# A streaming hybrid encoder step on one core: another way to turn and sum the conditioning half vectors of the feed-forward rounds

## The reference, cut to what matters

```
ada = (silu(c) @ w_ada + b_ada).reshape(B, 9, D)          # 9 sequences, D = 1024
x = x + 0.5 * ada[2] * SwiGLU1(modulate(rms(x), ada[0], ada[1]))
x = x + ada[5] * Mixer(modulate(rms(x), ada[3], ada[4]))
x = x + 0.5 * ada[8] * SwiGLU2(modulate(rms(x), ada[6], ada[7]))
y = modulate(rms(x), *(silu(c) @ w_ada_final + b_ada_final))
SwiGLU(x) = (silu(x @ w_gate) * (x @ w_up)) @ w_down       # inner width 2816
```

## Time and profile before

| | us |
|---|---|
| median of 3 runs | 2403.04 (2400.04 to 2405.37) |
| profiled execution, its own time | 2404.43 |
| profiled execution, span from first to last instruction | 2402.7 |
| TensorE busy | 2342.3 (97%) |
| VectorE busy | 1579.6 (66%) |
| ScalarE busy | 985.2 (41%) |
| GpSimd busy | 129.7 (5%) |
| mean granted TensorE clock | 0.987 of full |

### The profile page before, as it was taken

How to read it: one execution, slowest core, us unless ns; L and a number is a source line. 1 busy time by engine, 2 the same in 40 slices (tenths; PEclk the granted TensorE clock), 3 DMA queues, 4 the chain that set the end, 5 groups by cost and what they waited for, 6 DMA issues and landing times.

```text
span 2402.7 us, 31657 instructions
## 1 busy us (share of the span) xinstructions
PE 2342.3 (97%) x11530; PEld 2007.2 (84%) x11530; DVE 1579.6 (66%) x2530; ACT 985.2 (41%) x1701; POOL 129.7 (5%) x173
## 2 busy tenths in 40 slices
PE   6999999999999999999999999999999999999998
PEld 4677777787788787999999999997777788878887
DVE  5965665666666766655666565569666666666667
ACT  4544444444233443443344434235444444433335
POOL 0010101100000000101011110000010100000000
PEclk8999999999999999999999999999999999999998
DMA  9465455548855332321222213423645533497642
GB/s 347 158 202 179 159 178 189 165 164 302 341 214 187 130 125 89 120 57 45 65 65 62 61 38 112 150 81 102 210 158 177 186 129 127 159 379 276 236 140 82
DMA packets 247342, 381.02 MB, mean 159 GB/s; under 512 B 16689, under 2 KB 158185, under 8 KB 246070
## 3 DMA queue, kind: packets, MB, share of 16 engines
q1 hardware_dynamic: 234526, 345.15, 41.7%
q0 software_dynamic: 10240, 33.56, 4.5%
q10 hardware_dynamic: 2456, 0.75, 0.1%
HBM read 262.93 MB, written 116.47 MB: 158 GB/s over the span
## 4 chain that ended last, share of the span: by engine, by line
PE 83%; DVE 8%; DMA 3%; issue 2%; ACT 2%; SPq 0%; DVEq 0%; ACTq 0%
PE bank L535 25%; PE bank L537 24%; PE bank L536 24%; PE bank L2931 2%; PE bank L2928 2%; PE bank L2930 2%; DMA wraw<-in_w_ffn_down 2%; DVE u_lo L629 1%; PE bank L2814 1%; PE bank L2844 1%; DVE wraw L656 1%; DVE x L2263 1%; DVE x L1909 1%; DMA xrow<-in_x_prompt 1%; DMA wraw<-in_w_ffn_up 1%
## 5 line engine op out<-in xcount | busy, mean ns | idle before, releaser
L535 PE MATMUL bank<-ops,u_hi 128*128 128x512 f32 x1232 | 489.2, 397 | 9.2 <-DVE ops L1942 4.0
L629 DVE TENSOR_TENSOR u_lo<-wraw,u_hi 128x512 fp32r<-128x512 f32 (+2 forms) x532 | 315.4, 618 | 277.3 <-ACT u_hi L623 274.9
L537 PE MATMUL bank<-ops,u_lo 128*128 128x512 f32 x1232 | 482.0, 391 | 0.0
L536 PE MATMUL bank<-ops,u_hi 128*128 128x512 f32 x1232 | 481.6, 391 | 0.0
L623 ACT ACTIVATE u_hi<-wraw 128x512 fp32r<-128x512 f32 (+2 forms) x532 | 287.4, 568 | 278.0 <-PE bank L537 167.8
L535 PE MATMUL bank<-xn_hi,w_hi 128*128 128x384 f32 x1104 | 370.5, 336 | 5.2 <-ACT ww L1689 2.0
L537 PE MATMUL bank<-xn_hi,w_lo 128*128 128x384 f32 x1104 | 369.6, 335 | 0.0
L536 PE MATMUL bank<-xn_lo,w_hi 128*128 128x384 f32 x1104 | 369.4, 335 | 0.0
L535 PEld LDWEIGHTS bank<-ops,u_hi 128*128 128x128 f32 x1232 | 232.6, 189 | 86.4 <-issue 23.4
L537 PEld LDWEIGHTS bank<-ops,u_lo 128*128 128x128 f32 x1232 | 232.5, 189 | 49.7
L536 PEld LDWEIGHTS bank<-ops,u_hi 128*128 128x128 f32 x1232 | 232.8, 189 | 46.5
(11 more groups left out here) (320 smaller groups left out, 3959.0 us busy)
## 6 DMA issues: line engine op xcount, KB each, us to landing
h_dram<-stage_hi SPq DMA_DIRECT2D x154, 256.0 KB, 2.4
h_dram<-stage_lo SPq DMA_DIRECT2D x154, 256.0 KB, 2.7
ada_in<-in_w_ada POOLq DMA_DIRECT2D x96, 256.0 KB, 3.7
raw<-in_w_in SPq DMA_DIRECT2D x48, 512.0 KB, 4.8
wraw<-in_w_ffn_gate SPq DMA_DIRECT2D x44, 512.0 KB, 4.8
wraw<-in_w_ffn_up SPq DMA_DIRECT2D x44, 512.0 KB, 4.9
wraw<-in_w_ffn_down SPq DMA_DIRECT2D x48, 384.0 KB, 5.2
x<-x_dram SPq DMA_DIRECT2D x6, 2304.0 KB, 9.4
```

The costliest lines, as they stand in the source:

```text
L535: nc.tensor.matmul(out, hi, mov_hi, start=first, stop=False, skip_group_check=True)
L536: nc.tensor.matmul(out, hi, mov_lo, start=False, stop=False, skip_group_check=True)
L537: return nc.tensor.matmul(out, lo, mov_hi, start=False, stop=last, skip_group_check=True)
L629: nc.vector.tensor_tensor(unit(u_lo, f, g, u, n), unit_source(u, n), unit(u_hi, f, g, u, n).bitcast(F32), ALU.subtract).then_inc(u_lo_read ...
```

## The change

Four things are changed.

- The turn of the half vector's rows is done by four transposes, of full 128 columns, into the bank `WB[0]` (bank 2), in place of the four matmuls with `fold` into bank 7. It now stands behind `hidden_turn` and also waits for the first `join`, which has read bank 2.
- VectorE sums the four sides, by a `tensor_reduce` over 36 groups of four numbers from the bank into `ada`, waits for itself (`sides_summed`), and then adds the bias within `ada`.
- The parts are placed elsewhere. Part 0 of the next half vector stands right behind the turn (`half_begun`, `part`); part 1 stands behind S2[0]. The first half vector of each block has no turn ahead of it: its part 0 stays behind S1[0] of round 1, and its part 1 behind S2[0] of the same round.
- TensorE waits ahead of A12[0], the next writer of bank 2, until VectorE has added the half vector of the round before (`half_read`).

```
-PARTS_DONE = (5, 13)
-ROWS_FOLDED = 16
+def half_begun(f, g):
+    return half_of(f, g + 1) if g > 0 else []
...
                     for h in half_of(f, g):
                         dve.wait_ge(ada_folded, 2 * FIRST + h + 1)
                         o = FIRST * KT + 4 * h
+                        nc.vector.tensor_reduce(
+                            ada[:, o:o + 4, :],
+                            bank[WB[0]][:, :].rearrange("p (k a c) -> p k c a", k=4, a=SIDES)[:, :, 0:NSEQ, :],
+                            mybir.AxisListType.X, ALU.add).then_inc(sides_summed, 1)
+                        dve.wait_ge(sides_summed, h + 1)
                         nc.vector.tensor_tensor(
-                            ada[:, o:o + 4, :],
-                            bank[ADA_BANK][:, 0:4 * NSEQ].rearrange("p (k n) -> p k n", k=4),
+                            ada[:, o:o + 4, :], ada[:, o:o + 4, :],
                             badaT[:, o:o + 4].unsqueeze(2).broadcast_to([P, 4, NSEQ]), ALU.add)\
                           .then_inc(ada_ready, 1)
...
+                def part(h, r):
+                    pe.wait_ge(part_loaded, 16 * SIDES * (PARTS * h + r + 1))
+                    for s in range(SIDES):
+                        last = side(bank[ADA_BANK], r * SIDES + s, ada_in[s][:, :])
+                    last.then_inc(ada_mm, 1)
+
+                def rows_turned_over(g):
                     for h in half_of(f, g):
+                        pe.wait_ge(joined, of_round(f, g, 6, 1))
                         pe.wait_ge(ada_row_ready, 2 * FIRST + h + 1)
                         for b in range(4):
-                            o = b * NSEQ
-                            last = nc.tensor.matmul(bank[ADA_BANK][:, o:o + NSEQ], ada_row[:, b * P:(b + 1) * P],
-                                                    fold[:, :], start=True, stop=True)
+                            last = nc.tensor.transpose(bank[WB[0]][:, b * P:(b + 1) * P],
+                                                       ada_row[:, b * P:(b + 1) * P], ident[:, :])
                         last.then_inc(ada_folded, 1)
+
+                def half_read(g):
+                    for h in half_of(f, g):
+                        pe.wait_ge(ada_ready, 2 * FIRST + h + 1)
...
                     prompt(g, S1[0], O_T1, Z[0], True, False)
-                    parts(g, 5)
+                    if g == 1:
+                        pe.wait_ge(ada_ready, 2 * FIRST + HALVES[f][0])
+                        part(HALVES[f][0], 0)
...
                     prompt(g, S2[0], O_T2, X[0], False, False)
+                    for h in half_of(f, g):
+                        part(h, 1)
...
+                    half_read(g - 1)
                     prompt(g, A12[0], O_B21, W[0], True, True)
...
                     prompt(g, S3[0], O_T3, X[0], False, False)
-                    parts(g, 13)
...
                     prompt(g, A22[1], O_T4, X[1], False, True)
-                    parts(g, 16)
                     hidden_turn(g)
+                    rows_turned_over(g)
+                    for h in half_begun(f, g):
+                        part(h, 0)
...
+                    if rho == 0:
+                        half_read(ROUNDS - 1)
                     tile(A12[0], O_B21, W[0], True, True)
```

More of the change, by code:

```diff
@@ L443, in build @@
     ada_ready = sem("ada_ready")
+    sides_summed = sem("sides_summed")
     sp_step = sem("sp_step")
@@ L2937, in samples_in @@
                                 KH, bank[SAMPLE_BANK], h == 0)
-                def parts(g, event):
-                    for h in half_of(f, g):
[L2942 to L2951, removed]
+                def part(h, r):
[4 more added lines that the diff above has]
+                def rows_turned_over(g):
+                    for h in half_of(f, g):
+                        pe.wait_ge(joined, of_round(f, g, 6, 1))
                         pe.wait_ge(ada_row_ready, 2 * FIRST + h + 1)
                         for b in range(4):
-                            o = b * NSEQ
-                            last = nc.tensor.matmul(bank[ADA_BANK][:, o:o + NSEQ], ada_row[:, b * P:(b + 1) * P],
-                                                    fold[:, :], start=True, stop=True)
+                            last = nc.tensor.transpose(bank[WB[0]][:, b * P:(b + 1) * P],
+                                                       ada_row[:, b * P:(b + 1) * P], ident[:, :])
                         last.then_inc(ada_folded, 1)
+                def half_read(g):
+                    for h in half_of(f, g):
+                        pe.wait_ge(ada_ready, 2 * FIRST + h + 1)
                 def hidden_turn(g):
```

## The result

| us | before | after |
|---|---|---|
| median | 2402.33 (5 runs, 2400.04 to 2405.37) | 2414.24 (5 runs, 2413.39 to 2421.55) |
| ratio | | 1.0055 (95% interval 1.0044 to 1.0066) |
| span of the profiled execution | 2402.7 | 2411.7 |
| TensorE busy | 2342.3 (97%) | 2340.5 (97%) |
| VectorE busy | 1579.6 (66%) | 1585.3 (66%) |

The account below looks back on a forecast made before the run. TensorE was taken to bound the kernel, with 83% of the chain of waits. Turn -6.6, stalls +12.1 and clock +3.4 summed to +8.9 us, a median of 2411.9; range 2401.5 to 2416, the forecast's own 2407 to 2416.

Parts of the forecast that it names:

- The turn: At each half vector's turn, four transposes replace the fold matmuls: gain 0.41 us each, 6.6 us for 16.
- Part 0 next to the turn: Part 0 right behind the transposes saves nothing at its edges: 0, at most 1.5 us over 14 half vectors.
- The waits that cost nothing: New waits at the turn and ahead of A12[0], and VectorE's added reduce, stay hidden: 0, at most 16 x 0.1 us.
- The stall in block 0: Behind S2[0] of round 1, TensorE waits for part 1's last transfer: 8.0 us, between 4.9 and 8.8.
- up to 132 us the two programs do the same: Block 0, ahead of part 1's new place: nothing earlier is changed, so TensorE reaches it at 132.24 and POOL's pause stays.
- The stall in block 1: Behind S2[0] of round 1, TensorE waits for part 1's last transfer: 4.1 us, from below none.
- The clock: After each of the two stalls TensorE runs at the lower clock: 1.7 us each, 3.4 in all, between 0 and 3.8.
- POOL's pause: In block 0's round 1, POOL's issue stands 5.66 us between the seventh and eighth transfer, so the fourth is issued at 134.31.
- The loads land fast: Rival: round 1 loads land in 2.9 us in block 0, before TensorE comes in block 1; 2403.0; chance 0.17 with in-between states.
- The other two rivals: Round 1 stall never shows, 2396.4, chance 0.10; transposes at the turn cost as much as `fold`, 2418.5, chance 0.05.

Follow-up runs that it names:

- part 1 late: The changed kernel with part 1 of each block's first half vector put back behind S3[0] of round 1; 2400.32 us, ratio 0.9992.
- turn only: The kernel before with only the four transposes, the reduce and `half_read`, both parts at their old places; 2398.78 us, ratio 0.9989.
- part 0 ahead: The changed kernel with part 0 of each block's first half vector behind the turn of round 0; 2397.53 us, ratio 0.9985.
- the fold at the new place: The changed kernel with the four `fold` matmuls, into bank 2, in place of the transposes and the reduce; 2416.78 us, ratio 1.0055.
- the busy stall: The changed kernel with 24 and 16 unused matmuls ahead of the wait for part 1 in round 1; 2406.60 us, ratio 1.0019.

## Why the prediction was right, and where it was not

The median came out at 2414.2 against 2411.9, slower by 0.5% as forecast, for the reason that was given. In the profiled execution +9.0 us stand against +8.9.

- **The turn.** Predicted 0.41 a half vector and rounds of 46.66; measured 0.42 and 46.65. In the kernels without a stall the medians show only a part of the 6.6 us: 2.0 (part 1 late), 3.5 (turn only) and 4.8 (part 0 ahead). In the rounds all of it is there. The 2.7 us more of waits that the profiles with transposes have outside the rounds would fill most of the difference; the sum had them at nothing. Their cause stays open.
- **Part 0 next to the turn.** Predicted 0, bound 1.5; turn only has the same rounds to 0.02 us. Right. The fold gained 0.06 to 0.08 by its new place.
- **The waits that cost nothing.** VectorE's reduce took 0.30 us and the sum 0.20, near the lower end of the allowance:

```profile
L2039 DVE TENSOR_REDUCE ada<-bank x16: 300/303/304, 167.3 to 1956.0; 128x36 f32<-128x144 f32 x16
...
L2044 DVE TENSOR_TENSOR ada<-ada,badaT x16: 196/197/200, 167.6 to 1956.4; 128x36 f32<-128x36 f32 x16
```

  TensorE had no gap at the turn, at A12[0] or at S1[1] of any later round. Right.
- **The stall in block 0.** Predicted 8.0 (4.9 to 8.8); 5.8, 5.3 and 5.5 in three profiles, so this term was 2.2 to 2.7 us too large. The step that failed is "up to 132 us the two programs do the same". The programs do, but the executions did not: the profile of the kernel before had 1.93 us of idle time at 115.71 and then a lower clock, the first of the changed kernel 1.13 us and a full clock, and TensorE came to the place at 130.1 instead of 132.3. POOL's issues follow TensorE and came as much earlier. More important, the fourth transfer then went out ahead of the round's weight loads and not behind them. SP's timeline, the first load of weights in the changed kernel, then the three in the fold at the new place:

```profile
134.00 0.38 SPq L721 DMA_DIRECT2D wraw<-in_w_ffn_gate  x1
...
132.72 0.38 SPq L721 DMA_DIRECT2D wraw<-in_w_ffn_gate  x1
133.32 0.38 SPq L721 DMA_DIRECT2D wraw<-in_w_ffn_up  x1
134.28 0.37 SPq L721 DMA_DIRECT2D wraw<-in_w_ffn_gate  x1
```

  In the changed kernel POOL's fourth transfer (132.43) has 1.6 us of lead on the first of them and lands in 3.4; with the fold it is issued at 134.72, behind three, and lands in 6.6. Over the nine profiles that have this transfer at this place, it is ahead of the loads in six and lands in 3.4 to 4.1; it is behind two or three of them in three (the kernel before twice, and the fold) and lands in 6.6 to 7.0. The clock fell at 115 in just these three. There the idle time at 115 was 1.97 with a low clock, as in the profile of the kernel before, and the stall, 9.09 up to 141.40, is the 141.1 that was worked out from the earlier trace rows. So the sum was right for an execution like the one it was read from, and none of the three profiles of the changed kernel is such a one. Two of its first five runs lie 7 us above the others (2420.9 and 2421.6); they may be of that kind, but they have no profile.
- **The stall in block 1.** Predicted 4.1 (0 to 4.1); 4.0, 3.3 and 3.3. Right, and 0.8 smaller in two.
- **The clock.** Predicted 1.7 a stall; from the starts behind the stall 1.8 and 2.5 in the first profile, 2.5 and 1.5 in the second. Somewhat small. That the clock costs time at all, the busy stall shows by an experiment.
- **POOL's pause.** It stood between the seventh and the eighth transfer, as said. I took it for a fact of that place; it is a count, and its length is the landing of the seventh.
- **The balance.** In the first profile -6.7 (16 x 0.42), +9.8 (stalls) and +4.3 (clock) make +7.4 of the 9.0. The remaining 1.6 is the difference of larger things that were not in the sum: -2.4 for the shorter idle time at 115 with its full clock, +2.0 for longer waits for `slotF` and `slotH`, +1.2 for a lower clock behind one of them, and some +0.8 spread. That the total agreed to 0.1 is luck: the stalls were 2.3 less than the sum had them, the clock 0.9 more, and +1.6 came from what was not in it.
- **Rivals.** "The loads land fast" needed a landing under about 4 us in block 0. It was 3.4 to 3.6, and yet the time was not 2403. In block 0 the stall, 5.3 to 5.8, was indeed nearer to the rival's 4.9 than to the forecast's 8.0. But block 1's stall and its loss of clock, which the rival left out, were there (4.0 and 2.5 in the first profile). Its threshold stood on one term of three. The Trainium skill, "DMA: Bandwidth & Descriptors", section on the anatomy of one DMA on the GpSimd path, has a fit (2.0 us, and bytes over 436e3) by which 256 KB take an estimated 2.6 us; the quickest transfer of the changed kernel took 2.9 and the median 4.8, so the measurement decides. The other two rivals fell: the stall showed in every profile of the changed kernel, and the transposes cost 0.53 where the fold costs 0.89.

## What to carry to other kernels

A step that moves closer to the step before it needs its buffers earlier; where there is one set of buffers, look first at the places where the two steps are closest (here the first round of each block), and ask for issue, pause and landing of the last transfer there. In a program that is dense on TensorE such a wait costs more than its length, because the clock falls with it: 16 savings of 0.42 us were outweighed by two waits, and moving one part of each block ahead turned +12 us into -5. A landing time read from one execution belongs to the order of the transfers in that execution, so bound it by who else is in the queues, and not only by the row.

## What the runs showed of the hardware

- GpSimd's issue of transfers (256 KB each, onto 128 partitions) stands after each seventh, counted from its first one, until that one has landed and 0.4 us more. Landing and next issue are, in six places of five profiles, 132.0 and 132.43, 132.2 and 132.63, 134.3 and 134.72, 115.1 and 115.45, 142.1 and 142.51, 1700.7 and 1701.12. It holds in all twelve profiles: 166 pauses within groups of four, each behind a multiple of seven (up to 126) and 0.40 us past that landing, and no pause within a group anywhere else. They last 2.7 to 7.3 us. Moving the count by one or by four moved the pauses with it, across 1500 us of other work. Why it is seven, no run shows.
- One 256 KB transfer took 3.4 us ahead of three weight loads of 512 KB each and 6.6 behind them.
- The same idle time does not always cost the clock. The changed kernel's second profile has 2.11 us at 115.71 and goes on with starts 0.23 apart; the kernel before has 1.93 us there and starts 0.43 apart. Over six profiles with 1.86 to 2.13 us there, the clock held in three and fell in three. The three that held it had idled 1.16 to 1.33 us at about 80 us, the three that lost it 0.41 to 0.72; no run here separates that from other causes.
